# One encoder block on one core: experts' outputs added as whole rows, the last two blocks added in PSUM, a new order for the first blocks

## The reference

```python
def reference(x, meta_tokens, ..., final_norm):
    h = concat([meta_tokens, x])                       # 16 + 512 rows of 1024
    n = rmsnorm(h, attn_norm)
    ...                                                # attention of two kinds, one output projection
    h = h + mix @ w_out
    h = h + moe(rmsnorm(h, ffn_norm), w_router, b_router, w1, b1, w2, b2)
    h = rmsnorm(h, final_norm)
    return h[:, N_META:]                               # the 512 tokens

def moe(h, ...):                                       # top 4 of 32 experts for each token
    for each expert e and its tokens, with gates g:
        hu = x @ w1[e] + b1[e]                         # 1024 -> 2048
        gate, lin = minimum(hu[:1024], 7), clip(hu[1024:], -7, 7)
        act = gate * sigmoid(1.702 * gate) * (lin + 1)
        y = (act @ w2[e] + b2[e]) * g                  # 1024 -> 1024
        out[token] += y
```

## Time and profile before

| | us |
|---|---|
| runs: median, lowest, highest of 3 | 1395.08, 1393.59, 1397.64 |
| profiled execution, time | 1398.24 |
| profiled execution, span from first to last instruction | 1396.4 |
| mean granted TensorE clock (1 is 2.4 GHz) | 0.951 |
| TensorE matmuls busy | 1261.0 |
| VectorE busy | 590.6 |
| ScalarE busy | 245.7 |
| first up product of the experts to the last down product | 371.4 to 1372.5 |

### The profile page before, as it was taken

How to read it: one execution, slowest core, us unless ns; L and a number is a source line. 1 busy time by engine, 2 the same in 40 slices (tenths; PEclk the granted TensorE clock), 3 DMA queues, 4 the chain that set the end, 5 groups by cost and what they waited for, 6 DMA issues and landing times.

```text
span 1396.4 us, 35488 instructions
## 1 busy us (share of the span) xinstructions
PE 1261.0 (90%) x12994; PEld 566.6 (41%) x12995; DVE 590.6 (42%) x2076; ACT 245.7 (18%) x418; POOL 311.4 (22%) x475
## 2 busy tenths in 40 slices
PE   7999999989679985999899989995999699989982
PEld 4656666555223431443343324441443144434431
DVE  2113333663644441444345434451444244434444
ACT  2012223433101110111111101110111011101103
POOL 5310000002122221222222222221222122222221
PEclk9999999999799997999999989998999799999996
DMA  9520002508698999999999999999999999999996
GB/s 327 146 57 1 1 0 83 224 20 326 252 377 359 414 414 420 417 414 415 414 414 414 415 415 369 408 415 414 418 415 416 418 415 414 414 414 414 414 415 239
DMA packets 59632, 459.18 MB, mean 329 GB/s; under 512 B 8692, under 2 KB 19572, under 8 KB 35028
## 3 DMA queue, kind: packets, MB, share of 16 engines
q1 hardware_dynamic: 43268, 436.12, 75.5%
q0 software_dynamic: 15952, 22.36, 7.0%
q10 hardware_dynamic: 384, 0.31, 0.1%
HBM read 440.26 MB, written 18.51 MB: 329 GB/s over the span
## 4 chain that ended last, share of the span: by engine, by line
PE 73%; DMA 20%; DVE 3%; issue 2%; ACT 1%; DVEq 0%; POOL 0%; ACTq 0%; SPq 0%; POOLq 0%
PE PS L1689 34%; DMA sb_arena<-in_w 19%; PE PS L1716 16%; PE PS L1356 4%; PE PS L1362 4%; PE PS L1359 2%; PE PS L1360 2%; PE PS L1556 2%; PE PS L1696 1%; PE PS L1407 1%; PE PS L1529 1%; DMA xfd<-sb_arena 1%; PE PS L1459 1%; PE PS L1659 1%; PE PS L1505 1%
## 5 line engine op out<-in xcount | busy, mean ns | idle before, releaser
L1689 PE MATMUL PS<-sb_arena,sb_work 128*32 128x512 f32 x5184 | 602.1, 615 | 76.7 <-DMA sb_arena<-in_w 66.3
L1689 PEld LDWEIGHTS PS<-sb_arena,sb_work 128*32 128x32 f32 x5184 | 161.3, 112 | 442.5 <-issue 350.2
L1716 PE MATMUL PS<-sb_arena,sb_work 128*32 128x256 f32 x5184 | 296.7, 381 | 0.2 <-DMA sb_arena<-in_w 0.2
L1716 PEld LDWEIGHTS PS<-sb_arena,sb_work 128*32 128x32 f32 x5184 | 167.2, 111 | 107.7 <-issue 2.8
L1248 DVE TENSOR_SCALAR sb_work<-PS 128x256 f32<-128x256 f32 x81 | 34.3, 423 | 355.9 <-PE PS L1696 355.9
L822 ACT ACTIVATE PS<-sb_work 128x256 f32<-128x256 f32 x81 | 31.4, 388 | 854.4 <-DVE sb_work L1248 854.4
L625 POOL TENSOR_TENSOR sb_sm<-sb_sm 128x1 f32<-128x1 f32 x80 | 15.6, 195 | 621.6 <-DMA accd<-sb_work,sb_sidc 621.6
L598 POOL DMA_INDIRECT accd<-sb_work,sb_sidc x81 | 129.0, 1593 | 33.9 <-issue 33.1
L1159 DVE TENSOR_SCALAR sb_slots<-sb_ca,sb_b,sb_rk 128x128 bf16<-128x128 f32 x340 | 96.3, 354 | 59.3 <-issue 59.3
L831 ACT ACT_TABLE_LOAD x81 | 103.9, 1283 | 1.4
L1241 DVE STREAM_TRANSPOSE sb_work<-sb_work 128x256 f32<-128x256 f32 x81 | 53.5, 660 | 119.2 <-PE PS L1716 118.6
(11 more groups left out here) (259 smaller groups left out, 1032.5 us busy)
## 6 DMA issues: line engine op xcount, KB each, us to landing
sb_arena<-in_w SPq DMA_DIRECT2D x192, 2048.0 KB, 26.0
sb_arena<-in_w_in SPq DMA_DIRECT2D x6, 2048.0 KB, 21.0
sb_arena<-in_x SPq DMA_DIRECT2D x8, 512.0 KB, 7.9
sb_arena<-in_w_out SPq DMA_DIRECT2D x2, 2048.0 KB, 12.1
accd<-sb_arena SPq DMA_DIRECT2D x4, 512.0 KB, 9.1
xfd<-sb_arena SPq DMA_DIRECT2D x4, 512.0 KB, 6.5
sb_arena<-accd SPq DMA_DIRECT2D x4, 512.0 KB, 5.4
out<-sb_arena SPq DMA_DIRECT2D x4, 512.0 KB, 3.5
```

The lines of the kernel that those rows point to most:

```text
L1689: last = mm(PS[group(c), b, :].rearrange("p (a n) -> p a n", a=4), xT[:, k, :], w[:, k, :, c, :], start=k == 0, stop=False)
L1716: last = mm(PS[group(n), 4 + 2 * b, 0:QD], actT[:, k, :], w[:, k, n * QD:(n + 1) * QD], start=False, stop=k == KT - 1)
```

## The change

1. **Whole rows.** The sum is kept as 512 rows of 1024 (4 KB). `outputs` no longer leaves quarters on 128 partitions: each quarter is written to its quarter of 32 rows of 1024, so yb[b] is 32 partitions x 1024, and the scatter adds 32 rows of 4 KB. VectorE evicts quarters 0 and 1, ScalarE 2 and 3 (`high_outputs`). One more column is computed for the place in the sum (C_R).
2. **POOL.** Gather g + 3, scatter g and the wait for its landing follow one another.
3. **First blocks.** up 0, up 1, up 2, down 0, down 1, then up 3, down 2, up 4, down 3. A third selector serves up 2.
4. **Loads.** The first half of w2 of expert 0 and the last quarter of w1 of expert 1 are issued earlier in SP's order.
5. **The last two blocks** are not scattered. Their 64 rows stay in SBUF, a one-hot matrix of their tokens is made on VectorE, and 8 matmuls on TensorE put their sum for all 512 tokens into PSUM, which VectorE adds to the rows loaded from `accd`. Those rows are loaded once block nb - 3 has landed. POOL takes two of the multiplications by the gains.
6. **The end stands in the loops**, in the branch of the last block.

```diff
-        acc = nc.dram_tensor("accd", [Q * (T + SLOTS), QD], F32, kind="Internal").ap()
+        acc = nc.dram_tensor("accd", [T + SLOTS, D], F32, kind="Internal").ap()
-        yb = [work[:, (6 + b) * QD:(7 + b) * QD] for b in range(2)]
+        yb = [work[b * SLOTS:(b + 1) * SLOTS, 6 * QD:10 * QD] for b in range(2)]
+        yboth = work[0:2 * SLOTS, 6 * QD:10 * QD]
@@ SP
+                if t == TT - 2:
+                    sp.wait_ge(op_done, 2 * TT - 1)
+                    sp.dma_start(w2d(0, 0), w2v(0, 0)).then_inc(w2_full[0][0], 16)
...
                     sp.wait_ge(op_done, 2 * TT)
-                    sp.dma_start(w2d(0, 0), w2v(0, 0)).then_inc(w2_full[0][0], 16)
+                    w1_load(1, 3)
...
-            sp.wait_ge(up_done, nb)
+            sp.wait_ge(w1_read, 4 * ended + 3)
+            sp.dma_start(tokens, I["tokens"].to_broadcast([2 * SLOTS, T])).then_inc(acc_in, 16)
             sp.dma_start(fgain, I["final_norm"].to_broadcast([P, D])).then_inc(acc_in, 16)
-            sp.wait_ge(y_out, nb * 16)
+            sp.wait_ge(added, nb)
@@ POOL
+            def landed(n):
+                pool.wait_ge(added, n + 2)
+                pool.wait_ge(y_out, n * 16 + 16)
+                nc.gpsimd.tensor_tensor(sm[:, 21:22], ones1, ones1, ALU.mult).then_inc(added, 1)
...
+            def pass_on(g, b):
+                pool.wait_ge(xT_ready, g + 2)
+                gather(g + 3, 1 - b)
+                scatter(g, b)
+                landed(g)
@@ ScalarE
+            def high_outputs(n, b):
+                act.wait_ge(y_done, n + 1)
+                act.wait_ge(added, n + 1)
+                for c in (2, 3):
+                    rows = slice(c * SLOTS, (c + 1) * SLOTS)
+                    act.activation(yb[b][:, c * QD:(c + 1) * QD], PS[rows, 4 + 2 * b, 0:QD], ACT.Copy,
+                                   scale=gates[rows, bass.ds(n, 1)]).then_inc(y_high, 1)
@@ VectorE
-                nc.vector.tensor_scalar(yb[b], PS[:, 4 + 2 * b, 0:QD], gates[:, bass.ds(n, 1)], None, ALU.mult)\
-                    .then_inc(y_ready, 1)
+                for c in (0, 1):
+                    rows = slice(c * SLOTS, (c + 1) * SLOTS)
+                    nc.vector.tensor_scalar(yb[b][:, c * QD:(c + 1) * QD], PS[rows, 4 + 2 * b, 0:QD],
+                                            gates[rows, bass.ds(n, 1)], None, ALU.mult).then_inc(y_ready, 1)
...
+            def dve_block(g, b, i):
+                with dve.If(g + 1 < nb):
+                    hidden(g + 1, 1 - b, i + 1)
+                    slot_rows(g + 3, 1 - b, i + 2 if b else i + 1)
+                    turn_hidden(g + 1, 1 - b)
+                    outputs(g, b)
+                    slot_list(g + 4)
+                    selector(g + 2, b)
+                with dve.Else():
+                    last_places()
+                    outputs(g, b)
+                    final_norm()
@@ TensorE
+            def add_back():
+                pe.wait_ge(hot_ready, 1)
+                pe.wait_ge(y_ready, 3 * nb)
+                pe.wait_ge(y_high, 2 * nb)
+                for t in range(TT):
+                    for n in range(2):
+                        last = mm(PS[:, 2 * t + n, :], onehot[:, t * P:(t + 1) * P],
+                                  yboth[:, n * 512:(n + 1) * 512], start=True, stop=True)
+                    last.then_inc(back_done, 1)
...
+            up_of(2, second, 0, 2)
+            slot_product(4)
+            down(0, 0, 0, 0)
+            down_of(1, first, 1)
...
+            def pe_block(g, b):
+                here, following = places_of(g)
+                with pe.If(g + 1 < nb):
+                    up_of(g + 1, following, 1 - b)
+                    slot_product(g + 3)
+                    down_of(g, here, b)
+                with pe.Else():
+                    down_of(g, here, b)
+                    add_back()
```

More of the change, by code:

```diff
@@ L617, in _ @@
             gather(4, 0)
[L619 to L628, removed]
-                    pool.nop()
-            pool.wait_ge(xg_in[0], (nb + 5) // 2 * 16)
-            pool.wait_ge(xg_in[1], (nb + 4) // 2 * 16)
-            pool.wait_ge(y_out, nb * 16)
+            landed(0)
+            scatter(1, 1)
+            landed(1)
+            def pass_on(g, b):
[3 more added lines that the diff above has]
+                landed(g)
+            with pool.Fori(1, MAXBLK // 2) as i:
+                g = 2 * i
+                with pool.If(g + 2 < nb):
+                    pass_on(g, 0)
+                    with pool.If(g + 3 < nb):
+                        pass_on(g + 1, 1)
+                    pool.nop()
+                pool.nop()
+            pool.wait_ge(acc_in, 32)
+            for t in (0, 2):
+                pool.wait_ge(fin_sum, t + 1)
+                nc.gpsimd.tensor_tensor(fg[:, t, :], fh[:, t, :], fgain, ALU.mult).then_inc(fin_gain, 1)
+            pool.wait_ge(xg_in[0], (nb + 2) // 2 * 16)
+            pool.wait_ge(xg_in[1], (nb + 1) // 2 * 16)
         @block.scalar
@@ L824, in _ @@
             act.wait_ge(tab_ready, 1)
-            nb = act.value_load(btabi[0:1, NE - 1:NE], min_val=1, max_val=MAXBLK)
+            nb = act.value_load(btabi[0:1, NE - 1:NE], min_val=TOPK * T // SLOTS, max_val=MAXBLK)
             sigmoid(0, 0)
[L827 to L834, removed]
-                    act.nop()
@@ L836, in _ @@
[L836 to L846, removed]
+            sigmoid(1, 1)
@@ new lines, in final_rows, with final_norm @@
+            def final_rows(t):
+                nc.vector.scalar_tensor_tensor(fg[:, t, :], fh[:, t, :], rinv[:, t:t + 1], fgain, ALU.mult, ALU.mult)\
+                    .then_inc(fin_ready, 1)
+            def final_norm():
+                n0 = step.n
+                for t in range(TT):
+                    dve.wait_ge(back_done, t + 1)
+                    dve.wait_ge(x_in[t], 48)
+                    nc.vector.tensor_tensor(fh[:, t, :], PF[:, t * D:(t + 1) * D], fh[:, t, :], ALU.add)\
+                        .then_inc(fin_sum, 1)
+                dve.wait_ge(fin_sum, TT)
+                final_roots(0)
+                dve.wait_ge(fin_gain, 1)
+                nc.vector.tensor_scalar(fg[:, 0, :], fg[:, 0, :], rinv[:, 0:1], None, ALU.mult).then_inc(fin_ready, 1)
+                final_rows(1)
+                final_roots(2)
+                final_rows(3)
+                step.n = n0
@@ L1272, in _ @@
             slot_list(3)
+            hidden(1, 1, 1)
             slot_rows(3, 1, 1)
             slot_list(4)
[L1275 to L1289 removed]
@@ L1291, in _ @@
[L1291 to L1302 removed]
+            hidden(2, 0, 1)
```

216 lines of the change are left out of this document (138 added, 78 removed).

## The result

The change makes the kernel slower by more than half: 2183.98 us (median of 4 runs, 2168.42 to 2190.69) against 1394.34 us (4 runs, 1393.47 to 1397.64), ratio 1.564 with a 95% interval of 1.554 to 1.574. The forecast was 1370 us and its range closed at 1402. The profiled execution spans 2188.0 us.

A forecast was written before the change was run, and what follows sets the result against it. Bound by the expert weights' stream through all 16 DMA engines, TensorE close behind. Scatter 16 + gathers 1 + start 4 + end 4 = 25 us off 1396.4: 1371, or 1370 against the median 1395.1; range 1348 to 1402.

The forecast's parts named there:

- rival 3: TensorE's loop, 1120 to 1712 instructions, no longer stays in place and each pass stalls: 1540 to 1800 us; 15%.
- The steady block of 10.97 us: TensorE's time per block of 32 slots; claimed unchanged at 10.97 us, since product order stays from the fourth up product.
- The scatter term, 16 us: Adding each block's rows as 32 packets of 4 KB frees the weights' stream: 16 us saved, ends 2 and 43.
- 1 for the gathers: Three gathers fewer, gathering only to block nb: 1 us saved.
- The share: Software queue's (gathers and scatters) share of the engines in a steady stretch: falls from 9.8% to about 8.
- the landing: Time from a scatter's issue until its rows have landed beside the weights: falls from 10.8 us to about 6 to 7.
- rival 2: Pool queue's serial gather, scatter and wait for landing becomes the bound if landing stays at 10.8 us: 1490 us; 5%.
- The start, 4 us: New order of the first blocks and earlier loads release the third expert's weights sooner: 4 us gained, between about 0 and 7.
- The end, 4 us, with -3 as its low end: Last two blocks added back by TensorE instead of scattered: 4 us gained, ends -3 (products at low clock) and 6.
- Eviction by two engines, five steps in the slot list and the gather three blocks ahead: Extra eviction work and gathers are hidden behind TensorE's products; without cover the eviction would add 0.65 us a block.

The follow-up runs named there:

- short loop: Changed kernel with TensorE's down product written once instead of twice in each half of the loop: 1428.08 us, ratio 1.021 to the kernel before.
- 43 dead matmuls: Kernel before with 43 never-run matmuls behind a never-true test in each half of TensorE's loop: 1396.6 us, ratio 1.000.
- 64 dead matmuls: Also experiment 10: kernel before with 64 never-run matmuls in each half of TensorE's loop: 1401.74 us in one run.
- 85 dead matmuls: Also experiment 3: kernel before with 85 never-run matmuls behind a never-true test in each half of TensorE's loop: 2103.68 us, ratio 1.506.
- turned loop: Also experiment 4: short loop turned by half a block, its body starting with a down product, order of products unchanged: 1391.65 us, ratio 0.997 to the kernel before.
- 5: Kernel before with a second read of the table of places between down and up product in each half of the loop: 1397.9 us, ratio 1.002.
- experiment 6: Turned loop with the first blocks in the old order: 1388.29 us, ratio 0.995 to the kernel before.
- 7: Turned loop with all blocks scattered and the old end: 1392.47 us, ratio 0.998 to the kernel before.
- 8: Kernel before with only the rows of 4 KB and the eviction by two engines: 1393.87 us, ratio 0.999.
- 11: Turned loop with eight small matmuls ahead of the products that add the last rows: 1388.81 us, ratio 0.995 to the kernel before.
- 12: Turned loop with the old order of first blocks and eight small matmuls ahead of the adding products: 1388.22 us, ratio 0.996 to the kernel before.

## Why the prediction was wrong

**The step that failed.** It is the weight given to rival 3. The forecast's sum priced what the instructions do and left out where they lie; the doubled down product was counted (1120 to 1712) and then given 15%, and the sum had at nothing what measured 756 of the 790 us. Counted in the compiled kernels, waits and branches included, with four instructions for an fp32 `matmul` call (two matmul records and two weight loads in the trace) and two for a bf16 one, the loops are:

```
kernel                      matmuls and loads   all instructions   packets fetched   time, us
before                      1120                1168               19                1395
short loop                  1168                1221               22                1428
43 dead matmuls             1464                1514               21                1397
64 dead matmuls             1632                1682               21                1402 (one run)
after                       1712                1777               368               2184
85 dead matmuls             1800                1850               350               2104
```

The expectations above give 1,265, 1,332, 1,617, 1,785, 1,918 and 1,953 for these. They are 97 to 141 too high; 80 to 112 of that is what comes of taking the bf16 matmuls of the biases and slot products for four instructions as well. The order of the kernels is the same. The packets bear out the lower ones: TensorE's whole program has 19.4, 22.4, 20.8 and 21.4 times 256 instructions in the four kernels whose loop stays in place, and 19 to 22 packets are fetched, so each piece of code is fetched about once.

Up to 1682 the code stays in place, from 1777 on it is fetched in every pass: it is a threshold, and "half as long again as one that did" was no argument for 15% but for measuring the distance to it.

The Trainium skill (Runtime: NRT & Kernel Launch, Instruction fetch mechanics) has room for 2048 instructions in blocks of 256, and the prediction worked out from it, with an estimated 1,940, that the new loop would need a ninth block. The warning was right and the working was not: 1777 instructions touch eight blocks at most, wherever they start, and eight were said to have room, yet the loop was fetched anew. So the room that a loop can use is smaller than the prediction read out of the page, and the runs place it only between 1682 and 1777. Where in a block a loop begins, and how many blocks each touches, no run shows. The sentence of the Trainium skill on taken branches speaks of a window of two pages, which the prediction read as the whole room; with two pages the old loop would be fetched anew as well, and its 19 packets say that it was not. Of these 19, 13 came before the expert stage and 6 from 380 to 430 us, not all in the first pass, as the prediction has it.

**The size within rival 3** was off too: 1540 to 1800 us assumed one or two stalls of 6.5 us a pass. The loop does not lose one block of code, it loses all: 368 - 19 = 349 packets over 39.5 passes are 8.8 a pass, which is more than the 7 packets of 256 that 1777 instructions fill, and 756 us (after, less the short loop) are 19 us a pass, 2.2 us for each packet, the slower clock behind the pauses included.

**The steady block of 10.97 us** "from the fourth up product on" was wrong as the change stands, even with code in place. The order of the products is the old one, but the loop is cut at another place: its branches had stood after an up product, and stood now after a down product, whose matmuls are half as long. That was 36 us (short loop against turned loop). The prediction compared the products and not the sequencer's work between them.

**The scatter term, 16 us and 1 for the gathers.** The price was right: over the whole span the software queue took 7.0% of 1396.4, 97.8 us, and takes 5.9% of 1392.2, 82.1 us, in the turned loop; 15.6 less. The share came to 8.6% (8 forecast), the landing to 7.4 us (near 7 forecast), so rival 2 is out. What failed is the next half step, that a microsecond freed on the queue is a microsecond for the weights. From 430 to 1300 us the windows give this for the kernel before and for the one with whole rows alone (the last two numbers are the DMA share and GB/s):

```profile
430.00:1300.00 870.00, 806.76 (x9964) 316.80 (x9960) 377.35 (x1425) 118.64 (x142) 224.70 (x355) 0.96 1.02 413
```

```profile
430.00:1300.00 870.00, 814.84 (x10056) 316.95 (x10052) 457.08 (x1582) 186.75 (x286) 215.62 (x360) 0.98 1.01 416
```

That is 0.7% more, or 6 us of 870. The last down product ended at 1370.4 to 1374.3 us in four profiles with the old scatter (before, and experiments 3, 5 and 10) and at 1362.4 to 1369.3 in six with the new one (4, 6, 7, 8, 11, 12): means 1372.3 and 1366.8, 5.5 us where 21 were forecast with the start. The freed share was in part overlap between packets: the two queues' shares summed to 102.3% before. Counted from the first up product instead, the means are 1004.7 and 998.0 us, 6.8 us apart. Whether the rest is lost in the places where TensorE is the bound, I can't say from single profiles: the same old loop varies by 4 us from one to the next.

**The start, 4 us.** Nothing. In the turned loop the third up product began 22.5 us after the first (389.73 - 367.20), before 24.8 (396.26 - 371.44): it comes earlier by 2.3 us and not by 6, since it now waits for its own gathered rows, and it runs at the low clock. The fourth began 44.2 us after the first (411.40), against 42.4 before, and so the lead is gone. The wait had moved from the order to the data, and 3.21 us before the fourth were again for nothing that the profile names:

```profile
389.73 9.85 PE L1805 MATMUL PS<-sb_arena,sb_work 128*32 128x512 f32 x64 [3.67 <-DVE sb_work L1256]
```

**The end, 4 us, with -3 as its low end.** From the last down product to the end it was 24.1 us before, 20.1 in experiment 6 at full clock and 26.9 in experiment 4 at half. Both of the prediction's values were right; which of them holds changes from kernel to kernel, and perhaps from run to run. In the changed kernel itself the adding products ran at the low clock (13.1 us), and beside 790 us this term didn't matter.

**The rest held.** Eviction by two engines, five steps in the slot list and the gather three blocks ahead are as good as hidden: the turned loop has them all, and five blocks from 604.87 to 660.60 us take 11.15 us each, 0.2 more than the old 10.97 and still under the stream's 12.3.

The best version measured is the change with one down product in each half, the loop turned, and the old start: 1388.3 us (1388.2 with the eight small matmuls), 0.5% under the kernel before. That is all that the whole change holds.

## What to carry to other kernels

Before pricing what a rewritten loop does, count the instructions of its longest engine, both sides of every branch included, and compare with the longest loop that is known to stay in place; code that is written twice for a branch costs nothing until it costs everything. Where a loop is cut matters as well: put the reads and branches behind the engine's longest instructions. And a share of a queue is not time: when its packets shrink, measure the bytes per second of the stream beside it before booking the difference as gain.

## What the runs showed of the hardware

- TensorE's loop of 1682 instructions stayed in place (one run; one of 1514 in 8 runs), one of 1777 was fetched anew in each pass, all of it, in packets of 16 KB, with 2.1 to 2.2 us lost for each (756 us by 349 packets, 708 by 331, the slower clock included). The weights' stream beside it was then at 35% of the engines, so this is not a lack of DMA bandwidth.
- 682 more instructions in the loop, all but a test never executed, cost 708 us; 346 more cost nothing that could be told from the spread, and 514 more came to 1401.74 us in a single run, 7 us over the median beside it.
- A block's 32 rows added to memory as 32 packets of 4 KB took 0.69 us of the stream in place of 0.85 for 128 of 1 KB (6.1% of 1393.1 us against 7.0% of 1396.4, for the same 81 scatters).
- Shares of two busy queues sum to over 100%: 102.3% with many small packets, 101.1% with fewer. So a packet's time lies in part over another's.
- One read and two pairs of branches, put between a down and an up product, make TensorE stand for 0.65 to 1.11 us there (one run, from 430 us on). The read alone leaves about half the blocks without a pause and the others with mostly 0.15 to 0.36 us, 0.84 at most.
